# The opening of a macaron SwiGLU and attention block on one Trainium2 core: columns of c, scale and rstd made another way, and x turned once

## What is computed

```python
cond = silu(c)
ada = (cond @ w_ada + b_ada).reshape(b, 3, 3, 1024)      # w_ada is 1024 x 9216
shift, scale, gate = ada[:, :, 0], ada[:, :, 1], ada[:, :, 2]
rmsnorm(x, g) = x * rsqrt(mean(x * x) + 1e-6) * g
modulate(x, g, shift, scale) = rmsnorm(x, g) * (1 + scale) + shift

h = modulate(x, g_ffn1, shift[:, 0], scale[:, 0])
x = x + 0.5 * gate[:, 0] * swiglu(h, w_ffn1_up, w_ffn1_down)   # hidden width 2816
h = modulate(x, g_mix, shift[:, 1], scale[:, 1])
x = x + gate[:, 1] * (two kinds of attention over h @ w_in) @ w_out
h = modulate(x, g_ffn2, shift[:, 2], scale[:, 2])
x = x + 0.5 * gate[:, 2] * swiglu(h, w_ffn2_up, w_ffn2_down)
out = rmsnorm(x, g_final)
```

## Time and profile before

| what | us |
|---|---|
| median of 3 runs | 1105.65 |
| lowest and highest | 1104.77, 1109.12 |
| the profiled execution's own time | 1106.69 |
| its span in the trace | 1104.9 |
| PE busy in the span | 1080.8 (98%) |
| first product of a w_ffn1_up tile starts | 32.41 |
| the opening's 96 products of tiles 0 to 3 end | about 59.0 |

### The profile page before, as it was taken

How to read it: one execution, slowest core, us unless ns; L and a number is a source line. 1 busy time by engine, 2 the same in 40 slices (tenths; PEclk the granted TensorE clock), 3 DMA queues, 4 the chain that set the end, 5 groups by cost and what they waited for, 6 DMA issues and landing times.

```text
span 1104.9 us, 15937 instructions
## 1 busy us (share of the span) xinstructions
PE 1080.8 (98%) x5862; PEld 903.2 (82%) x5862; DVE 675.7 (61%) x997; ACT 496.9 (45%) x805; POOL 111.4 (10%) x100
## 2 busy tenths in 40 slices
PE   8999999999999999999999999999999999999997
PEld 5787888888877776889778777778999999988876
DVE  3745555555553446796886676669766766683333
ACT  5522223222222123775796676448445454541222
POOL 1000000000000001120011011000000000176350
PEclk9999999999999999999999999999999999999999
DMA  9756778867686772287599667145666766333221
GB/s 343 231 184 215 219 244 264 255 215 222 212 258 188 232 238 76 68 190 154 111 194 185 149 144 161 48 126 144 183 171 181 200 185 174 100 101 100 86 96 76
DMA packets 207720, 191.23 MB, mean 173 GB/s; under 512 B 6588, under 2 KB 182828, under 8 KB 205612
## 3 DMA queue, kind: packets, MB, share of 16 engines
q1 hardware_dynamic: 200064, 146.33, 45.4%
q0 software_dynamic: 7424, 44.04, 15.9%
q10 hardware_dynamic: 172, 0.06, 0.0%
HBM read 186.21 MB, written 44.04 MB: 208 GB/s over the span
## 4 chain that ended last, share of the span: by engine, by line
PE 82%; DVE 6%; DMA 5%; ACT 4%; issue 2%; SPq 0%; POOL 0%; DVEq 0%; ACTq 0%; POOLq 0%
PE bank L872 25%; PE bank L874 24%; PE bank L873 24%; DMA w_raw<-in_w_ffn_down_dram 3%; PE bank L1190 1%; PE bank L892 1%; ACT w_hi L1343 1%; PE bank L1162 1%; PE bank L1138 1%; DVE ada_acc L1830 1%; DMA w_raw<-in_w_ffn_up_dram 1%; PE bank L1139 1%; PE bank L925 1%; DMA k_hh_b<-k_hh_b 1%; PE bank L918 0%
## 5 line engine op out<-in xcount | busy, mean ns | idle before, releaser
L1811 DVE TENSOR_TENSOR w_lo<-w_raw,w_hi 128x1024 fp32r<-128x1024 f32 x99 | 121.2, 1225 | 177.2 <-ACT w_hi L1343 176.7
L872 PE MATMUL bank<-h_hi,w_hi 128*128 128x512 f32 x544 | 222.8, 410 | 0.3 <-DVE h_lo L1891 0.2
L873 PE MATMUL bank<-h_lo,w_hi 128*128 128x512 f32 x544 | 215.8, 397 | 0.0
L874 PE MATMUL bank<-h_hi,w_lo 128*128 128x512 f32 x544 | 215.8, 397 | 0.0
L1343 ACT ACTIVATE w_hi<-w_raw 128x1024 fp32r<-128x1024 f32 x99 | 104.6, 1058 | 214.7 <-PE bank L874 159.4
L872 PEld LDWEIGHTS bank<-h_hi,w_hi 128*128 128x128 f32 x544 | 103.0, 189 | 28.2 <-issue 4.2
L873 PEld LDWEIGHTS bank<-h_lo,w_hi 128*128 128x128 f32 x544 | 102.9, 189 | 26.1 <-issue 2.9
L874 PEld LDWEIGHTS bank<-h_hi,w_lo 128*128 128x128 f32 x544 | 102.7, 189 | 24.9
L1921 DVE TENSOR_TENSOR up_lo<-up_raw,up_hi 128x1024 fp32r<-128x1024 f32 x80 | 86.8, 1086 | 22.3 <-ACT up_hi L1423 22.3
L872 PE MATMUL bank<-combo,up_hi 128*128 128x256 f32 x320 | 90.5, 283 | 0.4 <-DVE kept_u L1928 0.4
L874 PE MATMUL bank<-combo,up_lo 128*128 128x256 f32 x320 | 90.6, 283 | 0.0
(11 more groups left out here) (274 smaller groups left out, 2203.0 us busy)
## 6 DMA issues: line engine op xcount, KB each, us to landing
w_sums<-in_w_ffn_up_dram POOLq DMA_DIRECT2D x24, 1280.0 KB, 9.0
ada_w<-in_w_ada_dram SPq DMA_DIRECT2D x56, 512.0 KB, 4.3
w_raw<-in_w_ffn_up_dram SPq DMA_DIRECT2D x48, 512.0 KB, 10.1
up_raw<-w_sums SPq DMA_DIRECT2D x40, 512.0 KB, 5.6
w_raw<-in_w_in_dram SPq DMA_DIRECT2D x28, 512.0 KB, 4.0
w_sums<-w_sums POOLq DMA_DIRECT2D x8, 1280.0 KB, 10.3
up_raw<-in_w_ffn_up_dram SPq DMA_DIRECT2D x20, 512.0 KB, 4.2
down_raw<-in_w_ffn_down_dram SPq DMA_DIRECT2D x20, 512.0 KB, 3.5
```

Source lines behind the costliest of these rows:

```text
L872: mm(dst, wh, xh, start=start, stop=False, skip_group_check=skip)
L873: mm(dst, wh, xl, start=False, stop=False, skip_group_check=skip)
L874: return mm(dst, wl, xh, start=False, stop=stop, skip_group_check=skip)
L1811: v.tensor_tensor(w_lo[:, s, :], w_raw[:, r, :], w_hi[:, s, :].bitcast(F32), ALU.subtract)\
```

## The change

c gets a transfer and a transpose of its own. Scale is made by `scale_product`, in which 128 x 128 blocks of w_ada are stationary and one column of cond moves, so that sums over k stand in PSUM as columns; `scale_line`, `keep_line` and `scale_columns` are gone. rstd is spread over partitions by four products of `ones` with a diagonal matrix of rstd; `xr_nat`, `xr`, `turn_xr`, `keep_xr` and `h_full` are gone, and h comes from `xT`, `amp` and `rstd`. SP takes SHIFT_A and SCALE_A by turns, then three tiles, then SCALE_B and SHIFT_B by turns with the fourth tile behind the first pair. Cut to its core:

```diff
-            load_piece(SHIFT_A)
-            load_piece(SCALE_A)
-            load_piece(SCALE_B)
+            for n in range(KC // 2):
+                load_piece(SHIFT_A, n)
+                load_piece(SCALE_A, n)
             for n in range(3):
                 load_up_first(n)
-            load_piece(SHIFT_B)
-            load_up_first(3)
+            for n in range(KC // 2):
+                load_piece(SCALE_B, n)
+                load_piece(SHIFT_B, n)
+                if n == 0:
+                    load_up_first(3)
...
-            def scale_row(p, k):
+            def scale_product(p, k):
 
                 if k % 2 == 0:
                     pe.wait_ge(piece_in[p][k // 2], 16)
-                last = mm(bank[4 + p][:], cond[:, k:k + 1].broadcast_to([P, P]), ada_first[:, p, k, :],
-                          start=k == 0, stop=k == KC - 1)
+                for j in range(4):
+                    last = mm(bank[SUM_BANK[p]][:, j:j + 1], ada_first[:, p, k, j * P:(j + 1) * P], cond[:, k:k + 1],
+                              start=k == 0 and j == 0, stop=k == KC - 1, skip_group_check=True)
                 if k == KC - 1:
-                    last.then_inc(row_up, 1)
-
-            def scale_columns(p):
-
-                pe.wait_ge(row_kept, p + 1)
-                for j in range(4):
-                    last = mm(bank[7 - 3 * p][:, j:j + 1], scale_line[0:1, p, j * P:(j + 1) * P], ones[0:1, :],
-                              start=True, stop=True)
-                last.then_inc(ada_col, 1)
+                    last.then_inc(ada_col, 1)
...
             pe.wait_ge(consts, N_IDENT)
-            warm(12)
+            warm(5)
+            pe.wait_ge(c_in, 16)
+            nc.tensor.transpose(bank[5][:, 0:KC], c_rows[0:KC, :], ident[0:KC, 0:KC]).then_inc(c_turned, 1)
+            warm(7)
...
-            for k in range(3):
-                turn_xr(k)
+            pe.wait_ge(consts, N_CONSTS)
+            pe.wait_ge(diag_r_done, TB)
+            for tb in range(TB):
+                last = mm(bank[6][:, tb * P:(tb + 1) * P], ones[:, 0:1].broadcast_to([P, P]), diag_r[:, tb, :],
+                          start=True, stop=True)
+            last.then_inc(rstd_up, 1)
             pe.wait_ge(cond_ready, 1)
+            pe.wait_ge(vec_cols, 1)
             for k in range(KC):
-                scale_row(SCALE_A, k)
-                if k < 3:
-                    turn_xr(k + 3)
-            pe.wait_ge(consts, N_CONSTS)
-            pe.wait_ge(xr_ready, 3)
+                scale_product(SCALE_A, k)
+                if k in (1, 3, 5):
+                    warm(3, 7)
             shift_columns(SHIFT_A)
-            scale_row(SCALE_B, 0)
-            scale_columns(SCALE_A)
-            for k in range(6, KC):
-                turn_xr(k)
-            for k in range(1, 6):
-                scale_row(SCALE_B, k)
+            warm(6, 7)
+            pe.wait_ge(x_upd, KC)
+            pe.wait_ge(rstd_kept, 1)
...
-            scale_row(SCALE_B, 6)
-            scale_row(SCALE_B, 7)
+            for k in range(4):
+                scale_product(SCALE_B, k)
             for k in range(4):
                 tile_chunk(T_UP1, 2, k, w2_hi, w2_lo)
-                if k == 2:
-                    scale_columns(SCALE_B)
+            for k in range(4, KC):
+                scale_product(SCALE_B, k)
             shift_columns(SHIFT_B)
...
+            act.dma_start(c_rows[0:KC, :], c.rearrange("o (r p) -> (o r) p", p=P)).then_inc(c_in, 16)
             act.wait_ge(vec_zero, 1)
...
+            act.wait_ge(c_turned, 1)
+            a(cond[:], bank[5][:, 0:KC], ACT.Exp, scale=-1.0).then_inc(cond_e, 1)
             for tb in range(TB):
...
+            act.wait_ge(rstd_up, 1)
+            a(rstd[:], bank[6][:], ACT.Copy).then_inc(rstd_kept, 1)
...
             for tb in range(TB):
-                v.tensor_scalar(xr_nat[:, tb, :], x_nat[:, tb, :], small[:, 20 + tb:21 + tb], None, ALU.mult)\
-                    .then_inc(xr_scaled, 1)
+                v.tensor_scalar(diag_r[:, tb, :], ident[:], small[:, 20 + tb:21 + tb], None, ALU.mult)\
+                    .then_inc(diag_r_done, 1)
```

More of the change, by code:

```diff
@@ L32 @@
 B_LOOP = 2
-XR_BANK = (5, 6, 7, 0, 1, 2, 3, 0)
+SUM_BANK = (4, 6, 5, 7)
 SCALE_A, SCALE_B, SHIFT_A, SHIFT_B = range(4)
@@ L908, in shift_columns @@
                 for j in range(4):
-                    last = mm(bank[4 + p - (p % 2) * 2][:, j:j + 1], ada_acc[:, p % 2 * SEQ + j * P:p % 2 * SEQ + (j + 1) * P],
+                    last = mm(bank[SUM_BANK[p]][:, j:j + 1], ada_acc[:, p % 2 * SEQ + j * P:p % 2 * SEQ + (j + 1) * P],
                               ones[:], start=True, stop=True)
@@ L1355, in _ @@
             nc.scalar.preload_act_table_set(EXP_LN_SET)
+            act.dma_start(c_rows[0:KC, :], c.rearrange("o (r p) -> (o r) p", p=P)).then_inc(c_in, 16)
             act.wait_ge(vec_zero, 1)
-            for src, row, rows in ((c, R_C, KC), (b_ada, R_BADA, NADA), (g_ffn1, R_G[0], KC), (g_mix, R_G[1], KC),
+            for src, row, rows in ((b_ada, R_BADA, NADA), (g_ffn1, R_G[0], KC), (g_mix, R_G[1], KC),
                                    (g_ffn2, R_G[2], KC), (g_sb_out, R_GO, SBJ), (g_fox_out, R_GO + SBJ, SBJ)):
@@ L1384, in _ @@
             a(vcol[:], bank[7][:, 0:P], ACT.Copy).then_inc(vec_cols, 1)
-            act.wait_ge(vec_cols, 1)
-            a(cond[:], col(R_C, KC), ACT.Exp, scale=-1.0).then_inc(cond_e, 1)
             for k in range(1, KC):
                 keep_x(k)
+            act.wait_ge(rstd_up, 1)
+            a(rstd[:], bank[6][:], ACT.Copy).then_inc(rstd_kept, 1)
             def make_rstd(s):
@@ L1503, in silu_first @@
                 a(tmp_a[:, f, :], bank[f][:], ACT.Silu).then_inc(silu_done, 1)
-            for k in range(6):
-                keep_xr(k)
-            keep_line(SCALE_A)
+            split_up(0)
             h_first(0)
-            keep_xr(6)
             h_first(1)
-            keep_xr(7)
-            split_up(0)
+            split_up(1)
             h_first(2)
-            split_up(1)
+            split_up(2)
             h_first(3)
-            split_up(2)
             split_up(3)
-            keep_line(SCALE_B)
             def hidden_high(f, j, hid0):
@@ L1882, in x_normed @@
                 n = KC * s + k
-                if k >= 4 and s == 1:
+                if k >= 4 and s < 2:
                     dve.wait_ge(h_done, n - 3)
@@ L2034, in _ @@
                 piece_product(SHIFT_A, k)
-            piece_sum(1, 0, 6)
-            piece_sum(2, KC, 7)
+            dve.wait_ge(vec_cols, 1)
+            piece_sum(1, KC, SUM_BANK[SCALE_A])
             first_amp(0)
-            dve.wait_ge(amp_done, 1)
-            dve.wait_ge(ada_out, 2)
-            h_full(0)
-            h_full(1)
+            x_first(0)
+            piece_sum(2, 0, SUM_BANK[SHIFT_A])
+            x_first(1)
+            split_up(0)
             h_low_first(0)
             h_low_first(1)
-            h_full(2)
-            split_up(0)
+            x_first(2)
+            split_up(1)
             h_low_first(2)
-            split_up(1)
-            h_full(3)
+            x_first(3)
+            split_up(2)
             h_low_first(3)
@@ L2051, in _ @@
                 piece_product(SHIFT_B, k)
-            split_up(2)
+            split_up(3)
             for k in range(4, KC):
                 piece_product(SHIFT_B, k)
-            split_up(3)
-            piece_sum(3, KC + 4, 4)
+            piece_sum(3, KC + 4, SUM_BANK[SCALE_B])
             first_amp(1)
-            piece_sum(4, 4, 5)
-            dve.wait_ge(amp_done, 2)
-            dve.wait_ge(ada_out, 4)
-            h_full(4)
-            h_full(5)
+            x_first(4)
+            piece_sum(4, 4, SUM_BANK[SHIFT_B])
+            x_first(5)
             h_low_first(4)
+            x_first(6)
             h_low_first(5)
-            h_full(6)
+            x_first(7)
             h_low_first(6)
-            h_full(7)
             h_low_first(7)
```

73 lines of the change are left out of this document (22 added, 51 removed).

## The result

| | before | changed |
|---|---|---|
| median on the same chip, 12 runs each, us | 1105.43 | 1115.32 |
| lowest and highest | 1103.39, 1109.12 | 1109.16, 1117.40 |
| the profiled execution: own time, span | 1106.69, 1104.9 | 1115.97, 1114.2 |
| mean granted clock of that execution | 0.997 | 0.986 |
| first product of a tile starts | 32.41 | 30.48 |

The ratio is 1.0076, 95% interval 1.0059 to 1.0094. The change makes the kernel slower by 0.8%, 8.4 us by the ratio (6.5 to 10.4). The forecast was 1106.6 us, its range ended at 1110.0 us, and slower by over 0.5% had a chance of 0.06.

A forecast was written before the change was run, and what follows sets the result against it. PE, busy 98% of the span, was taken to bound the kernel: 19.9 us removed, 20.9 added, 0.4 off and 0.3 for c give +0.9 us on 1105.65, so 1106.6 us. The 8-in-10 range was 1103.2 to 1110.0 us.

The forecast's parts named there:

- The ledger: PE's work list from 7 to 59 us: 19.9 us removed, 20.9 us added, +0.6 us after 0.4 us off.
- rstd's spreading: Four float32 products of 128 columns on PE in the opening, spreading rstd over partitions; booked at 0.9 us.
- Waits of PE: New waits of PE for DVE around the first tile: 1.7, 1.1 and 1.0 us, together 3.8 us.
- The chain over DVE: DVE's steps after T up to the first h_lo, 3.8 us, of which PE fills 2.1 us.
- a late landing: c's transfer landing at 6 us or later delays squares, rstd and warming: +1.5 to +2.5 us, 1108 us; chance 0.08.
- the sum's own range: Range of the forecast sum, 1104.7 to 1108.9 us, from cheaper or dearer products, c wait and spreading; chance 0.60.
- The step that failed: the clock: PE's clock was expected at 1.00 through 30 to 50 us, since sixteen one-column passes had run at 1.00.
- The signs that the prediction named for being wrong: Blocks above 0.9 us, products 0.42 us apart after one-column blocks, c wait over 1 us, opening's end before 57 us.
- the rival: PE's clock falls at waits or single-column blocks: one fall gives 1108.2 us, three 1111.4 us; chance 0.20.
- DMA at nothing: The new order of transfers in the opening was costed at nothing, covered by PE's own work.
- T: The end of SCALE_A's last product on PE, forecast near 22.5 us.
- Early tile: Without PE's 3.8 us of waits the opening ends 3 to 6 us sooner: 1100 to 1103.5 us; chance 0.12.

The follow-up runs named there:

- e1_wide: The changed kernel with 128 equal moving columns instead of one in every scale_product matmul; 1107.67 us, ratio 1.0003.
- e6_old_loads: e1_wide with SP's transfers in the old order (SHIFT_A, SCALE_A, SCALE_B, three tiles, SHIFT_B, fourth tile); 1110.99 us, ratio 1.0032.
- e5_filled: e1_wide without the nine warm products between SCALE_A's products, two SCALE_B products put into PE's waits, their piece loaded behind tile 0; 1103.77 us, ratio 0.9972.
- e9_scale_first: e5_filled with each piece of SCALE_A loaded ahead of SHIFT_A's; 1101.78 us, ratio 0.9969.
- e7_old_c: e1_wide with c back among the small vectors and twelve warm products without a stop; 1108.13 us, ratio 1.0002.

## Why the prediction was wrong, point by point

**The ledger: right in sum, partly by luck.** It forecast +0.9 us at the full clock, first tile near 26.5 us, end near 59.9 us. e1_wide, which has the change's list and the clock at 1.00, has 27.54 and 59.99 us and a ratio of 1.0003. The first tile is 1.0 us late and the end agrees because terms offset each other: e1_wide's products cost 0.90 us, 1.6 us more in sum than booked, against 0.5 us of waits and 0.3 us for c that did not come; some 0.7 us of the agreement stays unresolved. Its terms:
- A `scale_product` was taken at 0.80 us from `shift_columns`; it measured 0.85 us in the changed kernel. Sixteen make 13.6 us, 0.8 us more. By that row, 0.106 us a pass, the price was 6% low. The 107 ns per load that the prediction quoted from the Trainium skill, page TensorE: Matmul & The Clock Gate, section LDWEIGHTS, make an estimate of 0.86 us for eight passes; the trace agrees, 0.85 us.
- rstd's spreading: 14.58 - 13.69 = 0.89 us against 0.9.
- Waits of PE: 1.7, 1.1 and 1.0 us forecast, 1.93, 0.72 and 0.69 us in e1_wide. The chain over DVE was right in kind and 0.5 us long in sum.
- c: 0.3 us were booked for a late landing. PE turned c at 4.49 us with no idle time in the row. That rival is out.
- Two slips that change no conclusion: SCALE_B behind the first tile is eight products, 32 blocks, not sixteen, though its 6.4 us are right; and the low end of the sum's own range comes to 1105.0 us from the terms named (0.8, 0.3 and 0.5 us), not 1104.7.

**The step that failed: the clock.** The forecast carried PE's clock at 1.00 through the opening, with the reason that "from 24.0 to 27.5 us sixteen one-column passes ran with the clock at 1.00". Those passes stood in two groups of eight beside wide products; the change has 64 of them in SCALE_A alone. A row of a short mixed stretch was carried over to a much longer one. Its list of places where the clock might fall had the first wait and the two blocks of SCALE_B; SCALE_A, with single columns from 14.58 us on and nine fillers between, was not on it, and that is where the clock fell first, between 20 and 21 us, and stayed down up to the first product of tile 0. Beyond that stretch the trace of before had no row for it, so this was an unknown to bound, and it got 0.20. What the runs showed in its place: 12.0 us of full-clock time lost in the opening, in all twelve executions a lower mean clock than any of the kernel before, and, with 128 equal moving columns instead of one, a clock of 1.00 and an opening that ends 9.3 us sooner (e1_wide). The signs that the prediction named for being wrong were the right ones: blocks above 0.9 us (1.64) and products 0.42 us apart behind single columns (0.43).

**The price of the rival was mis-sized too.** A fall was costed at eight products of 0.2 us, 1.6 us, from the earlier trace rows, so even three falls gave 1111.4 us. In the changed kernel the windows add up to 12.0 us lost, of which about 2 us fell into waits that PE has at the full clock (3.3 us in e1_wide, 1.5 us here). 59.99 us, less 0.8 us for the cheaper single columns, plus 10.2 us is 69.4 us; 69.25 us was found. The lower level stayed through the single-column products (0.54 and 0.58 over whole windows of 10 us) and for 5.7 us of wide products behind the last of them. The price is the length of all the work for which the clock stays down, not of the few products behind a pause.

**DMA at nothing: half right.** The order by turns was costed at nothing. In the changed list it's worth about 4.3 us of the opening (e6_old_loads, a fall of the clock included), since it is what lets tile 0 start early. The ledger's sum was right only because it had counted T and DVE's chain with tile 0's parts in time, and never asked what the old order would have cost. SCALE_A's last piece was put at 18 to 20 us by counting transfers; in e5_filled PE stood until 21.43 us for it. The fillers hid that in the changed list, where PE wanted the piece at 22.42 us. Nor is the order by turns the best one (e9_scale_first).

**Early tile.** That rival needed the waits gone. e5_filled and e9_scale_first do it in small, by moving SCALE_B's products into the waits: 58.19 and 57.13 us. It lies in the list, but the change's own order doesn't take it.

## What to carry to other kernels

Count TensorE's clock as a term of the sum wherever a change replaces wide moving operands with single columns, and price it by the whole work that would run at the lower level. Where each matmul loads new weights, the moving side can be made 128 columns wide for 0.05 us per four matmuls, and with that the loss was gone here (ratio 1.0003 against 1.0076), where bf16 fillers between did not help (1.0071). It does not guard against a fall behind a wait (e7_old_c). A first tile that may start earlier is worth its start only if the transfers are ordered by who waits first and its waits are filled with work that is due anyway.
